# Another order of the opening among three engines, and the last expert's rows placed tile by tile at the layers' boundary and in the tail

## The chip, the cores and the metric

The kernel runs on one core of a Trainium2 chip. The time is the device time in microseconds of one execution; lower is better. In the traces PE is TensorE, DVE VectorE, ACT ScalarE, POOL GpSimd and SP the engine that issues most DMAs.

## The reference

Two layers of a decoder trunk over x (512 tokens x 1024), float32, then a final RMSNorm. Each layer is a mixer (retention and pooling branches behind one input projection) and a mixture of 16 experts, of which each token uses two; both see a normed x, scaled and shifted by rows computed from a condition c.

```python
for l in range(DEPTH):                       # DEPTH = 2
    mod = cond @ w_ada[l] + b_ada[l]
    sh1, sc1, g1, sh2, sc2, g2 = jnp.split(mod, 6, axis=-1)
    h = modulate(rmsnorm(x, norm1_g[l]), sh1, sc1)
    x = x + g1[:, None, :] * mixer(h, ...)
    h = modulate(rmsnorm(x, norm2_g[l]), sh2, sc2)
    x = x + g2[:, None, :] * moe(h, ...)     # top 2 of 16 experts, each silu(h@gate)*(h@up) @ down
return rmsnorm(x, final_g)
```

## The kernel before, in words

Tokens are four tiles of 128 rows (t = 0 to 3). Weights come as a stream of pieces of 128 x 1024 float32 (512 KB) into eight slots of `raw`. ScalarE copies a piece to `w_hi` (`hi`, L642; in experts `hi_e`, L820), VectorE subtracts it from the piece to get `w_lo` (`lo`, L989; `lo_e`, L1487), and TensorE makes each product in three passes of high and low parts (L1733 to L1735). Activations are split likewise (`unit_hi_half` L684, `unit_lo_half` L1087). `w_hi` and `w_lo` have four slots, and during the experts four more (`w_hi_more`, `w_lo_more`), which lie over `hT`. A piece of next use waits for `w_used`, the count of pieces that TensorE is done with. `LEAD` says how many pieces of an expert are converted before it begins.

Every engine has its own program in order, written by hand; what ties them together are semaphores. VectorE's `drain` waits until its own writes are in place.

Opening of layer 0: four columns of the modulation rows are products of `cond` with weights (`first_column` L2058, `first_fold` L2065) in the order 2, 0, 3, 1; the x tiles are normed in two halves of 512 columns (`first_scaled`, `first_shifted`), transposed, split (`first_hi`, `first_lo`) and multiplied with the pieces of group q (`first_product`).

Experts: each has 12 pieces, eight of gate and up (n = 0 to 7) and four of down (8 to 11), and 6 matmuls a piece. `hidden`, `hidden_transposes` and `hidT` carry the hidden rows from one to the other. `rows_out` scales an expert's output rows into `y_out` (L1510), and GpSimd stores them with an indirect DMA to `y_rows` (L2223). Of the last expert nothing is stored: its rows are added by a matmul with a 0/1-like matrix `slot_last` (transposed from `hot_last`, L1947, copied by ScalarE at L959), `last_rows_added` (L1959). What the other experts gave to each token comes back by DMA as pairs of rows (`pairs_load`, L533 to L541) once all stores have landed: `pair_early` for tiles 0 and 1, `pair_2`, `pair_3`. VectorE adds them to x (`combine`, two instructions of L1559 each); tile 2's pairs are added by TensorE (`pair_matmuls`, L1966). Then VectorE adds TensorE's sum of last rows (`last_add`, L1572) and counts `x_final`.

Boundary: x of each tile is squared and summed by ScalarE (`row_deviations`, L646, L648), normed and shifted by VectorE (`norm_tile`, L1035, L1074, L1076), transposed by TensorE (`norm_transposes`, L1818, two units of four transposes a tile), split, and multiplied with group q tile by tile (`group_tile`: 4 pieces x 2 x 3 = 24 matmuls a tile). Before, all last rows and pairs are done in one block ahead of the boundary, and the transposes of tile t + 1 stand in the middle of tile t. Tail: after layer 1 the same adds, then the final norm (`normed_output`, L1584) and the stores of `out` (L584).

## Time and profile before

| | us |
|---|---|
| median of three runs | 1492.13 (1491.58 to 1492.9) |
| the profiled execution | 1491.59 |
| its span in the trace | 1489.9 |
| PE busy | 1445.9 (97%) |
| DVE busy | 1134.2 (76%) |
| ACT busy | 773.7 (52%) |
| mean DMA rate | 253 GB/s |

The span is the time from the first to the last recorded instruction or transfer. PE's share says how much of the span TensorE had a matmul under way; what is left of it are waits. A timeline row gives start, duration, engine, line, what was written from what, how often in a row, and in square brackets the idle time before it with the instruction whose end released it.

### The profile page before, as it was taken

To read this page: it belongs to the slowest core of one execution; us is meant where nothing else is said; L and a number is where in the kernel's file an instruction comes from. 1 tells how busy PE (TensorE), PEld (TensorE's weight loads), DVE (VectorE), ACT (ScalarE), POOL (GpSimd) and SP (SyncE) were. 2 spreads that over 40 slices of the span, in tenths; PEclk is the share of its full clock that TensorE was granted. 3 is DMA by queue.
4 is the path that set the end of the run, shared out by engine and by line. 5 is a ranking of instruction groups with operands and counts; after the bars stand their busy time and mean duration, and the time that the engine had idled before them with its cause. 6 is when DMAs were issued, how large, how long until landed. Compare 5 with 4: busy or idle time off the path is not lost.

```text
span 1489.9 us, 18810 instructions
## 1 busy us (share of the span) xinstructions
PE 1445.9 (97%) x6824; PEld 1157.3 (78%) x6824; DVE 1134.2 (76%) x1531; ACT 773.7 (52%) x1102; POOL 141.6 (10%) x139
## 2 busy tenths in 40 slices
PE   6999999999999999999989999999999999999996
...
GB/s 332 296 185 200 159 220 193 147 184 161 193 210 250 386 391 387 388 389 379 313 226 197 192 141 114 194 143 89 85 171 154 295 274 394 398 387 394 380 353 190
DMA packets 107269, 377.49 MB, mean 253 GB/s; under 512 B 16505, under 2 KB 16697, under 8 KB 106404
## 3 DMA queue, kind: packets, MB, share of 16 engines
...
## 4 chain that ended last, share of the span: by engine, by line
PE 82%; DVE 12%; ACT 1%; DMA 1%; issue 1%; DVEq 1%; ACTq 0%; SPq 0%
PE ps L1733 25%; PE ps L1735 24%; PE ps L1734 24%; DVE w_lo L1487 4%; DVE w_lo_more L1487 3%; PE ps L1818 2%; PE ps L1985 1%; DMA raw<-w 1%; PE ps L1887 1%; PE ps L2032 1%; DVE xgT_lo L1476 1%; PE ps L1891 1%; DVE y_out L1510 1%; DVE w_lo L989 0%; PE ps L1959 0%
## 5 line engine op out<-in xcount | busy, mean ns | idle before, releaser
L989 DVE TENSOR_TENSOR w_lo<-raw,w_hi 128x1024 fp32r<-128x1024 f32 x134 | 163.7, 1224 | 216.6 <-ACT w_hi L642 215.2
L642 ACT ACTIVATE w_hi<-raw 128x1024 fp32r<-128x1024 f32 x134 | 141.1, 1058 | 332.8 <-PE ps L1735 332.8
L1487 DVE TENSOR_TENSOR w_lo<-raw,w_hi 128x1024 fp32r<-128x1024 f32 x192 | 229.3, 1217 | 6.1 <-ACT w_hi L820 5.0
L1733 PE MATMUL ps<-w_hi,hT_lo 128*128 128x512 f32 x512 | 206.9, 404 | 7.0 <-DVE hT_lo L1087 6.9
L820 ACT ACTIVATE w_hi<-raw 128x1024 fp32r<-128x1024 f32 x192 | 197.9, 1058 | 27.8 <-DMA raw<-w 14.8
L1487 DVE TENSOR_TENSOR w_lo_more<-raw,w_hi_more 128x1024 fp32r<-128x1024 f32 x168 | 200.5, 1216 | 2.5 <-ACT w_hi_more L820 1.6
L1735 PE MATMUL ps<-w_hi,hT_hi 128*128 128x512 f32 x512 | 201.1, 393 | 0.0
L1734 PE MATMUL ps<-w_lo,hT_hi 128*128 128x512 f32 x512 | 200.7, 392 | 0.0
L820 ACT ACTIVATE w_hi_more<-raw 128x1024 fp32r<-128x1024 f32 x168 | 172.8, 1057 | 19.2 <-DMA raw<-w 16.7
L1733 PE MATMUL ps<-hT_hi,w_lo 128*128 128x512 f32 x320 | 130.5, 408 | 0.0
L1735 PE MATMUL ps<-hT_hi,w_hi 128*128 128x512 f32 x320 | 125.0, 390 | 0.0
L1734 PE MATMUL ps<-hT_lo,w_hi 128*128 128x512 f32 x320 | 124.7, 390 | 0.0
L1733 PEld LDWEIGHTS ps<-w_hi,hT_lo 128*128 128x128 f32 x512 | 97.0, 189 | 31.7 <-DVE hT_lo L1087 9.0
L1733 PE MATMUL ps<-w_hi,xgT_lo 128*128 128x512 f32 x288 | 114.3, 397 | 3.1 <-DVE xgT_lo L1476 2.1
L1735 PEld LDWEIGHTS ps<-w_hi,hT_hi 128*128 128x128 f32 x512 | 96.8, 189 | 21.0
L1735 PE MATMUL ps<-w_hi,xgT_hi 128*128 128x512 f32 x288 | 112.4, 390 | 0.0
L1734 PE MATMUL ps<-w_lo,xgT_hi 128*128 128x512 f32 x288 | 112.3, 390 | 0.0
L1734 PEld LDWEIGHTS ps<-w_lo,hT_hi 128*128 128x128 f32 x512 | 97.0, 189 | 18.8 <-issue 0.2
L1001 DVE SCALAR_TENSOR_TENSOR ada_acc<-raw,cond,ada_acc 128x512 f32<-128x512 f32 x140 | 104.9, 749 | 6.3
L2223 POOL DMA_INDIRECT y_rows<-y_out,idx x30 | 58.0, 1932 | 436.0 <-DVE y_out L1510 418.8
L1733 PE MATMUL ps<-w_hi_more,xgT_lo 128*128 128x512 f32 x224 | 88.5, 395 | 0.0
L1735 PE MATMUL ps<-w_hi_more,xgT_hi 128*128 128x512 f32 x224 | 87.4, 390 | 0.0
...
## 6 DMA issues: line engine op xcount, KB each, us to landing
...
```

Of the source, the lines that this page charges most:

```text
L642: act.activation(w_hi[:, q % W_SLOTS], stream_piece(l, q, r), ACT.Copy).then_inc(w_hi_ready, 1)
L820: act.activation(ring_hi(r), expert_piece(e, n), ACT.Copy).then_inc(w_hi_ready, 1)
L989: v.tensor_tensor(w_lo[:, q % W_SLOTS], stream_piece(l, q, r), w_hi[:, q % W_SLOTS], ALU.subtract).then_inc(raw_used, 1)
L1001: one = v.scalar_tensor_tensor(ada_acc[:, acc], piece, c, ada_acc[:, acc], ALU.mult, ALU.add)
L1476: v.tensor_tensor(xgT_lo[:, slot, cols], ps[:, 4 + j], xgT_hi[:, slot, cols], ALU.subtract).then_inc(xgT_lo_ready, 1)
L1487: v.tensor_tensor(ring_lo(e * EXP + n), expert_piece(e, n), ring_hi(e * EXP + n), ALU.subtract).then_inc(raw_used, 1)
L1510: v.tensor_tensor(y_out[:, before % 2].rearrange("p (h n) -> p h n", h=2), ps[:, 2:4], gate_row[:].rearrange("p (h n) -> p h n", h=2), ALU ...
L1733: pe.matmul(dst, a_lo, b_hi, start=start, stop=False)
L1734: pe.matmul(dst, a_hi, b_lo, start=False, stop=False)
L1735: return pe.matmul(dst, a_hi, b_hi, start=False, stop=stop)
L1818: one = pe.transpose(bank[:, i * P:(i + 1) * P], src[:, i * P:(i + 1) * P], ident)
L2223: pool.indirect_dma_start(y_rows, bass.IndirectOffsetOnAxis(ap=idx[:, e:e + 1], axis=0), y_out[:, e % 2], None, bounds_check=2 * T - 1, oo ...
```

## The change

- Opening: ScalarE, VectorE and TensorE keep their instructions, in another order. Pieces 2 and 3 are converted earlier; column 1 is computed before product (0,2,1); the first transposes of the second half stand before product (0,3,1).
- Last expert: six instead of four of its pieces are converted during it. Its last four pieces go to ring slots 6, 7, 2, 3, so that slots 0 and 1 of `w_hi` and `w_lo` are free; in layer 0 the first two pieces of layer 1 are converted into them (`early_high`, `early_low`). `last_hot` comes earlier, the transposes of `hot_last` go into the middle of the down product, `combine` of tile 0 before `last_rows_out`.
- SP issues the first four loads of layer 1 before the pair loads; these wait for an earlier piece.
- Boundary: last rows of tiles 0 and 1 come first; pairs, the transposes of tile 0 and last rows of tile 2 next; last rows of tile 3 between the dense tiles 0 and 1. The PSUM banks of the sums change with it (`ADD_BANK`). `combine` of tiles 1 and 3 is cut into halves that stand between other steps; no `drain` and separate count follow the adds.
- Tail: the same halves of `combine`; the last tile's final norm and its store are made in two halves of 512 columns.

```diff
@@ -127,12 +127,16 @@
 RING_FROM, RING_TO = RAW_SLOTS + AHEAD, EXP * NE - W_SLOTS
-LEAD = [W_SLOTS, W_SLOTS] + [min(W_SLOTS + e - 1, 2 * W_SLOTS) for e in range(2, NE)] + [0]
+RING_END = (6, 7, 2, 3)
+LEAD = [W_SLOTS, W_SLOTS] + [min(W_SLOTS + e - 1, 2 * W_SLOTS) for e in range(2, NE - 1)] + [2 * W_SLOTS - 2, 0]
+EARLY = 2
...
-    return p % (2 * W_SLOTS) if RING_FROM <= p < RING_TO else p % W_SLOTS
+    if p >= RING_TO:
+        return RING_END[p - RING_TO]
+    return p % (2 * W_SLOTS) if p >= RING_FROM else p % W_SLOTS
...
@@ -489,8 +494,8 @@
         PAIR_DMAS = (16, 16, 16, 32)
-        ADD_BANK = (0, 4, 6, 2)
-        PAIRS_AT = 0
+        ADD_BANK = [(0, 2, 6, 6)] * (DEPTH - 1) + [(0, 2, 6, 2)]
+        PAIRS_AT = W_SLOTS
@@ -533,7 +538,7 @@
                     sp.wait_ge(row_stored[p], (l + 1) * STORED[p])
-                sp.wait_ge(w_used, w_done(l, MIX + RING_TO - W_SLOTS - 1))
+                sp.wait_ge(w_used, w_done(l, MIX + RING_TO - 7))
@@ -579,10 +584,14 @@
             pairs_load(DEPTH - 1)
-            for t in range(NT):
+            for t in range(NT - 1):
...
                 sp.dma_start(out[t * P:(t + 1) * P], x[:, t]).then_inc(out_stored, 16)
-            sp.wait_ge(out_stored, 16 * NT)
+            for half in range(2):
+                cols = slice(512 * half, 512 * half + 512)
+                sp.wait_ge(norm_done, NT + half)
+                sp.dma_start(out[(NT - 1) * P:NT * P, cols], x[:, NT - 1, cols]).then_inc(out_stored, 16)
+            sp.wait_ge(out_stored, 16 * (NT + 1))
...
@@ -640,6 +649,13 @@
                 act.activation(w_hi[:, q % W_SLOTS], stream_piece(l, q, r), ACT.Copy).then_inc(w_hi_ready, 1)
+            def early_high(l, q):
+                r = RAW_OF_W[q]
+                act.wait_ge(landed[r % RAW_SLOTS], land_value(l, r))
+                act.wait_ge(w_used, l * PROD + (q + 1) - W_SLOTS)
+                act.activation(w_hi[:, q % W_SLOTS], raw[:, r % RAW_SLOTS], ACT.Copy).then_inc(early_hi, 1)
@@ -830,14 +846,24 @@
                 if last:
+                    hi_e(next(pieces))
+                    hi_e(next(pieces))
+                    hi_e(next(pieces))
...
                     hi_e(next(pieces))
-                    hi_e(next(pieces))
                     hidT(0)
-                    hi_e(next(pieces))
+                    if l < DEPTH - 1:
+                        for q in range(EARLY):
+                            early_high(l + 1, q)
...
                     sig(1)
+                    hi_e(next(pieces))
                     hidT(1)
+                    if l < DEPTH - 1:
+                        act.drain().then_inc(w_hi_ready, EARLY)
+                    act.activation(spare[:], k("eps"), ACT.Sqrt)
+                    act.wait_ge(hot_last_turned, l + 1)
+                    act.activation(slot_last[:], ps[:, 4].rearrange("p (a b) -> p a b", a=NT), ACT.Copy).then_inc(slot_last_ready, 1)
@@ -883,33 +909,27 @@
             first_row_copy(0)
+            first_hi(0, 0)
             hi(0, 1, RAW_OF_W[1])
-            first_hi(0, 0)
...
             first_hi(0, 3)
+            hi(0, 2, RAW_OF_W[2])
             first_row_copy(3)
+            hi(0, 3, RAW_OF_W[3])
             first_row_copy(1)
-            hi(0, 2, RAW_OF_W[2])
-            first_hi(1, 0)
-            hi(0, 3, RAW_OF_W[3])
-            for t in range(1, NT):
+            for t in range(NT):
...
                 if l:
+                    for q in range(EARLY, W_SLOTS):
+                        hi(l, q, RAW_OF_W[q])
...
                         row_deviations(t)
-                        if t == 0:
-                            hi(l, 0, RAW_OF_W[0])
-                        if t == 1:
-                            hi(l, 2, RAW_OF_W[2])
-                            hi(l, 3, RAW_OF_W[3])
                         norm_hi(l, "h1", t)
-                        if t == 0:
-                            hi(l, 1, RAW_OF_W[1])
@@ -953,10 +973,8 @@
                         act.wait_ge(ov_y, b * 16 + 16)
+                        act.activation(spare[:], k("eps"), ACT.Sqrt)
                 act.nop()
-                act.activation(spare[:], k("eps"), ACT.Sqrt)
-                act.wait_ge(hot_last_turned, l + 1)
-                act.activation(slot_last[:], ps[:, 4].rearrange("p (a b) -> p a b", a=NT), ACT.Copy).then_inc(slot_last_ready, 1)
@@ -989,6 +1007,11 @@
+            def early_low(l, q):
+                v.wait_ge(early_hi, (l - 1) * EARLY + (q + 1))
+                v.tensor_tensor(w_lo[:, q % W_SLOTS], raw[:, RAW_OF_W[q] % RAW_SLOTS], w_hi[:, q % W_SLOTS], ALU.subtract)
@@ -1521,15 +1544,23 @@
                     rows_out(e - 1)
+                    lo_e(next(pieces))
+                    lo_e(next(pieces))
+                    last_hot(l)
...
                     hidT(0)
-                    lo_e(next(pieces))
+                    if l < DEPTH - 1:
+                        for q in range(EARLY):
+                            early_low(l + 1, q)
...
                     hidden(1)
+                    lo_e(next(pieces))
                     hidT(1)
-                    last_hot(l)
+                    if l < DEPTH - 1:
+                        v.drain().then_inc(raw_used, EARLY)
+                    combine(l, 0)
@@ -1559,30 +1590,25 @@
-            def combine(l, t, complete=False):
+            def combine(l, t, parts=(0, 1)):
...
                 v.wait_ge(pair_in[t], (l + 1) * PAIR_DMAS[t])
-                weighted_pair(t, w_early)
-                if complete:
-                    v.sem_inc(x_final, 1)
-            def last_add(l, t, complete=True):
+                weighted_pair(t, w_early, parts)
+            def last_add(l, t):
...
                 v.wait_ge(last_added, l * NT + (t + 1))
-                one = v.tensor_tensor(x[:, t].rearrange("p (h n) -> p h n", h=2), ps[:, ADD_BANK[t]:ADD_BANK[t] + 2],
-                                      x[:, t].rearrange("p (h n) -> p h n", h=2), ALU.add)
-                if complete:
-                    one.then_inc(x_final, 1)
-                else:
-                    v.drain()
+                v.tensor_tensor(x[:, t].rearrange("p (h n) -> p h n", h=2), ps[:, ADD_BANK[l][t]:ADD_BANK[l][t] + 2],
+                                x[:, t].rearrange("p (h n) -> p h n", h=2), ALU.add).then_inc(x_final, 1)
...
                 inverse_deviation(DEPTH * 8, t)
-                v.scalar_tensor_tensor(x[:, t], x[:, t], x_rs[:, t:t + 1], scale_row[:], ALU.mult,
-                                       ALU.mult).then_inc(norm_done, 1)
+                for cols in ([slice(0, D)] if t < NT - 1 else [slice(0, 512), slice(512, D)]):
+                    v.scalar_tensor_tensor(x[:, t, cols], x[:, t, cols], x_rs[:, t:t + 1], scale_row[:, cols], ALU.mult,
+                                           ALU.mult).then_inc(norm_done, 1)
@@ -1593,51 +1619,50 @@
                     lo(0, 0, RAW_OF_W[0])
+                    first_lo(0, 0)
                     first_shifted(0, 1)
-                    first_lo(0, 0)
...
                     first_scaled(0, 2)
+                    first_lo(0, 1)
                     first_shifted(0, 2)
-                    first_lo(0, 1)
...
                     first_part_rows(1)
+                    lo(0, 2, RAW_OF_W[2])
...
                     first_scaled(1, 0)
+                    first_shifted(1, 0)
                     first_scaled(1, 1)
-                    first_shifted(1, 0)
-                    lo(0, 2, RAW_OF_W[2])
+                    lo(0, 3, RAW_OF_W[3])
...
                     first_shifted(1, 1)
-                    lo(0, 3, RAW_OF_W[3])
                     for t in (2, 3):
+                        first_scaled(1, t)
                         first_lo(1, t - 1)
-                        first_scaled(1, t)
...
                 else:
-                    combine(l - 1, 0)
+                    combine(l - 1, 1, [0])
                     last_add(l - 1, 0)
-                    last_add(l - 1, 1, False)
+                    combine(l - 1, 1, [1])
                     norm_tile(l, 0, "h1", 0)
-                    combine(l - 1, 1, True)
-                    lo(l, 0, RAW_OF_W[0])
+                    last_add(l - 1, 1)
+                    lo(l, 2, RAW_OF_W[2])
                     norm_lo(l, "h1", 0)
-                    lo(l, 1, RAW_OF_W[1])
-                    lo(l, 2, RAW_OF_W[2])
...
                     norm_lo(l, "h1", 1)
-                    combine(l - 1, 3)
+                    combine(l - 1, 3, [0])
                     norm_tile(l, 0, "h1", 2)
+                    combine(l - 1, 3, [1])
+                    norm_lo(l, "h1", 2)
                     last_add(l - 1, 3)
-                    norm_lo(l, "h1", 2)
@@ -1711,14 +1736,15 @@
             last = DEPTH - 1
-            combine(last, 0)
+            combine(last, 1, [0])
             last_add(last, 0)
-            combine(last, 1)
+            combine(last, 1, [1])
...
             normed_output(0)
-            combine(last, 3)
+            combine(last, 3, [0])
...
             last_add(last, 2)
+            combine(last, 3, [1])
@@ -1795,7 +1821,7 @@
                 for j in range(GROUPS[g][1]):
-                    if g == 0 and t < NT - 1 and j == 2:
+                    if g == 0 and t == 1 and j == 3:
@@ -1940,30 +1966,37 @@
-            def last_rows_added(l):
+            def hot_last_turn(l):
...
                 one.then_inc(hot_last_turned, 1)
-                pe.wait_ge(slot_last_ready, l + 1)
-                pe.wait_ge(z_half, l + 1)
-                for t in range(NT):
-                    if t == 2:
-                        pe.wait_ge(pair_in[2], (l + 1) * PAIR_DMAS[2])
-                        pair_matmuls(0)
-                        pair_matmuls(1)
-                    for half in range(2):
-                        if t == 0 and half == 1:
-                            pe.wait_ge(y_copied, l * NE + (NE + 1))
-                        one = pe.matmul(ps[:, ADD_BANK[t] + half], slot_last[:, t], y_out[:, (NE - 1) % 2, 512 * half:512 * half + 512],
-                                        start=t != 2, stop=True)
-                    one.then_inc(last_added, 1)
+            def last_rows(l, t):
+                if t == 0:
+                    pe.wait_ge(slot_last_ready, l + 1)
+                    pe.wait_ge(z_half, l + 1)
+                if t == 3:
+                    pe.wait_ge(x_final, (l + 1) * NT + (3 if ADD_BANK[l][3] == ADD_BANK[l][2] else 2))
+                for half in range(2):
+                    if t == 0 and half == 1:
+                        pe.wait_ge(y_copied, l * NE + (NE + 1))
+                    one = pe.matmul(ps[:, ADD_BANK[l][t] + half], slot_last[:, t], y_out[:, (NE - 1) % 2, 512 * half:512 * half + 512],
+                                    start=t != 2, stop=True)
+                one.then_inc(last_added, 1)
+            def last_rows_pairs(l):
+                pe.wait_ge(pair_in[2], (l + 1) * PAIR_DMAS[2])
+                pair_matmuls(0)
+                pair_matmuls(1)
...
                 for half in range(2):
-                    pe.matmul(ps[:, ADD_BANK[2] + half], diag_w[:, j], pair_2[:, j, 512 * half:512 * half + 512],
+                    pe.matmul(ps[:, ADD_BANK[0][2] + half], diag_w[:, j], pair_2[:, j, 512 * half:512 * half + 512],
@@ -2019,6 +2052,8 @@
                             hidden_transposes(1)
+                            if last:
+                                hot_last_turn(l)
@@ -2086,15 +2121,15 @@
             first_transposes(0, 3)
-            first_product(0, 2, 1)
-            first_fold(3)
...
             first_column(1, [2, 3])
+            first_fold(3)
+            first_product(0, 2, 1)
+            first_fold(1)
             first_product(0, 3, 0)
-            first_fold(1)
+            first_transposes(1, 0)
             first_product(0, 3, 1)
-            first_transposes(1, 0)
@@ -2106,10 +2141,17 @@
                 if l:
+                    last_rows_pairs(l - 1)
                     norm_transposes(l, 0)
+                    last_rows(l - 1, 2)
...
                         group_tile(l, 0, t)
+                        if t == 0:
+                            norm_transposes(l, 1)
+                            last_rows(l - 1, 3)
+                        if t == 2:
+                            norm_transposes(l, 3)
@@ -2153,6 +2195,7 @@
                     pe.wait_ge(y_copied, l * NE + (NE + 1))
+                    pe.wait_ge(slot_last_ready, l + 1)
@@ -2184,7 +2227,12 @@
                 pe.nop()
-                last_rows_added(l)
+                last_rows(l, 0)
+                last_rows(l, 1)
+                if l == DEPTH - 1:
+                    last_rows_pairs(l)
+                    last_rows(l, 2)
+                    last_rows(l, 3)
```

## Rows read from the trace of the kernel before

**Rows 1.** The page: busy time of TensorE; the chain that ended last, by engine.
```profile
PE 1445.9 (97%) x6824; PEld 1157.3 (78%) x6824; DVE 1134.2 (76%) x1531; ACT 773.7 (52%) x1102; POOL 141.6 (10%) x139
...
PE 82%; DVE 12%; ACT 1%; DMA 1%; issue 1%; DVEq 1%; ACTq 0%; SPq 0%
```
**Rows 2.** Waits of TensorE over the whole span: total us, times, longest.
```profile
PE ps L1733 <- DVE hT_lo L1087: 6.9, 3, 2.5
...
PE ps L1818 <- DVE h_nat L1076: 3.9, 1, 3.9
PE ps L2032 <- DVE hid L1493: 3.0, 9, 0.7
...
PE ps L1733 <- DVE hidT_lo L1499: 0.9, 3, 0.3
```
**Rows 3.** Timeline of TensorE in the opening: start, duration, operation, idle before.
```profile
25.00 0.50 PE L1733 MATMUL ps<-w_hi,hT_lo 128*128 128x512 f32 x1 [2.19 <-DVE hT_lo L1087]
...
47.96 0.50 PE L1733 MATMUL ps<-w_hi,hT_lo 128*128 128x512 f32 x1 [2.45 <-DVE hT_lo L1087]
```
**Rows 4.** Timelines of ScalarE and of SP's DMA issues in the opening.
```profile
22.68 1.05 ACT L642 ACTIVATE w_hi<-first_w 128x1024 fp32r<-128x1024 f32 x1
...
44.50 0.60 ACT L870 ACTIVATE shift_row<-ps 128x512 f32<-128x512 f32 x1 [4.48 <-DVE h_nat L1059]
45.00 1.05 ACT L642 ACTIVATE w_hi<-raw 128x1024 fp32r<-128x1024 f32 x1
...
35.15 7.01 SPq L522 DMA_DIRECT2D raw<-w  x6
```
**Rows 5.** Timeline of TensorE at the boundary between the layers.
```profile
744.03 3.70 PE L1959 MATMUL ps<-y_out,slot_last 128*128 128x512 f32 x8 [0.69 <-ACT slot_last L959]
...
757.71 0.50 PE L1733 MATMUL ps<-w_hi,hT_lo 128*128 128x512 f32 x1 [2.24 <-DVE hT_lo L1087]
...
764.63 1.97 PE L1818 MATMUL ps<-const,h_nat 128*128 128x128 f32 x8 [3.88 <-DVE h_nat L1076]
...
781.09 0.48 PE L1733 MATMUL ps<-w_hi,hT_lo 128*128 128x512 f32 x1
...
789.12 0.39 PE L1735 MATMUL ps<-w_hi,hT_hi 128*128 128x512 f32 x1
```
**Rows 6.** Busy time by stretch; then granted clock, DMA share and GB/s.
```profile
764.00:768.00 4.00, 3.37 (x12) 3.08 (x13) 3.14 (x5) 1.96 (x3) 0.00 (x0) 0.50 0.40 152
768.00:772.00 4.00, 4.00 (x14) 3.11 (x14) 3.35 (x4) 0.56 (x3) 0.00 (x0) 0.72 0.01 2
```
**Rows 7.** VectorE: timeline at the boundary, then groups with mean ns of one.
```profile
744.15 2.64 DVE L1559 SCALAR_TENSOR_TENSOR x<-pair_early,w_early,x 128x1024 f32<-128x1024 f32 x2
...
751.34 1.23 DVE L1076 TENSOR_TENSOR h_nat<-h_nat,shift_row 128x1024 f32<-128x1024 f32 x1
...
L1572 DVE TENSOR_TENSOR x<-ps,x 128x1024 f32<-128x1024 f32 x8 | 9.6, 1219 | 0.2
...
L1487 DVE TENSOR_TENSOR w_lo<-raw,w_hi 128x1024 fp32r<-128x1024 f32 x192 | 229.3, 1217 | 6.1 <-ACT w_hi L820 5.0
```
**Rows 8.** Pair loads of layer 0 with their landing; GpSimd's timeline of row stores.
```profile
L538 SPq DMA_DIRECT2D pair_early<-y_rows x2: 381/426/471, 733.3 to 733.7; - x2
...
DMA to landing us min/median/max: 4.7/5.8/6.9
...
714.42 2.66 POOL L2223 DMA_INDIRECT y_rows<-y_out,idx  x1 [15.04 <-DVE y_out L1510]
729.86 0.96 POOL L2223 DMA_INDIRECT y_rows<-y_out,idx  x1 [12.78 <-DVE y_out L1510]
```
**Rows 9.** Timeline of VectorE in the tail.
```profile
1467.78 2.65 DVE L1559 SCALAR_TENSOR_TENSOR x<-pair_early,w_early,x 128x1024 f32<-128x1024 f32 x2
...
1483.86 0.16 DVE L1035 RECIPROCAL x_rs<-x_std 128x1 f32<-128x1 f32 x1 [0.45 <-ACT x_std L648]
...
1485.53 1.28 DVE L1584 SCALAR_TENSOR_TENSOR x<-x,x_rs,scale_row 128x1024 f32<-128x1024 f32 x1
```

5 lines of the change are left out of this document (3 added, 2 removed).

## The prediction

> **What bounds the kernel now.** I read the page first: TensorE is busy for 97% of the span and carries 82% of the chain that ended last, VectorE 12% [rows 1]. So TensorE's work sets the time, except where it waits and where it has finished. The change adds and removes no matmul, so all it can move is idle time of TensorE, half-clock time of TensorE, and the piece of VectorE's work behind the last matmul. The list of TensorE's waits [rows 2] shows what there is: 6.9 us for `hT_lo` and 3.9 us for `h_nat`, both of the opening and of the boundary between the layers, and small ones of the last expert (`hid`, `hidT_lo`). The timelines then place them. Times below are positions in the profiled execution.
>
> **Opening.** Two waits stand before first uses of `hT_lo`: 2.19 us until 25.00 and 2.45 us until 47.96 [rows 3].
> - The first. ScalarE converts piece 1 (22.68, 1.05 us) before it copies the first transposed unit; VectorE likewise makes `h_nat` of tile 1 before its own half of that unit [rows 4]. The edit turns both around. The transposes end near 22.8, ScalarE's copy of 0.6 us then ends near 23.55, VectorE's subtract of 0.7 near 24.25, and the first product starts at 24.3: 0.7 us gained. Piece 1 is then converted by 24.55 and its low part by 26.0; it is needed after two transposes and six matmuls, near 26.4. Nothing is late.
> - The second. ScalarE copies the shift row at 44.50, then piece 2 at 45.00 [rows 4], then the transposed unit; VectorE repeats that order with 1.22 us for the low part. In the new kernel pieces 2 and 3 are converted while ScalarE waits for column 3 and column 1 anyway (it is idle 4.5 us before 44.50), and TensorE runs column 1 before product (0,2,1) and puts product (0,3,1) behind the transposes. I lay the new order out from 36.2: column 1 (1.9 us) to 38.0, fold 3 to 38.9, product (0,2,1) to 40.3, fold 1 to 41.2, product (0,3,0) to 42.6, transposes to 43.0, product (0,3,1) to 44.35. VectorE is ready with the unit's low half at 44.8, so the next product starts at 44.85 against 47.96: 3.1 us in all, the first 0.7 among them. The weak point is piece 2: SP issues its load when column 3's third piece is used, 34.4 in the new order (35.15 before [rows 4]). It needs to land by 38; behind it in ScalarE's queue stands the copy of the scale row, and behind that the whole second half. Bounds for this part: 0.7 (the load is late) to 3.8 (VectorE never late). I take 3.1.
>
> **Last expert, both layers.** Two of expert 14's conversions move behind `rows_out`, so expert 14's rows are scaled 2.3 us earlier (two of 1.217 [rows 7]). `hidT_lo` no longer stands behind two conversions: its three waits add up to 0.9 us [rows 2], of which 0.5 in the tail, and there the wait for `hid` (0.26 of the 3.0) goes too. The four transposes of `hot_last` (0.6 us) move between the matmuls of the down product; they are issued in either case, but now `slot_last` is copied long before it is needed. In layer 0 the two early conversions cost VectorE 2 x 1.217 in the same place, so `hidden(1)` ends at 738.4 as now and the down product at 742.8 as now: nothing gained, nothing lost. In the tail they are absent, and the down product ends 0.85 us earlier.
>
> **Boundary.** Now: the last rows and pairs are three blocks like the one at 744.03, 3.4 us each, up to 754.4; then transposes, 2.24 us wait, half of a dense tile, 3.88 us wait for the next `h_nat`, and then matmuls at half clock: the granted clock is 0.50 in 764 to 768 and 0.72 in 768 to 772 [rows 5, 6]. The group ends at 789.3. A matmul costs (789.12 - 781.09) / 35 = 0.229 us at full clock, a tile of 24 costs 5.5.
> The new order, from the down product's end at 742.8. VectorE: combine of tile 0 (two of 1.32 us [rows 7]) lies before `last_rows_out`, in a place where it now waits for TensorE's last product; `last_rows_out` ends at 744.15 as now; then half of combine 1 to 745.4, last add 0 (1.219 less overlap, 1.15) to 746.65, ScalarE's deviation 1.6 us beside the other half of combine 1, norm of tile 0 to 751.2 (now 752.57 [rows 7]), last add 1 to 752.3, low part of piece 2 to 753.45, `norm_lo` to 754.7. TensorE: last rows 0 and 1 from 743.7 (0.3 earlier, it waits for the first half of `y_out` only) to 747.15, pairs to 750.6, 0.7 idle, transposes 0 to 752.2, last rows 2 to 753.9, 0.85 idle, dense tile 0 from 754.75 to 760.2 (now from 757.71). Transposes 1 need the norm of tile 1, ready 758.7: no wait. Last rows 3 (1.7 us) need last add 2, done 759.8: no wait, and they cover `norm_lo` of tile 1. Tile 1 runs 762.9 to 769.25 with transposes 2 in it, 0.4 idle, tile 2 to 775.1, transposes 3, then 1.75 idle, since nothing is left to cover the copy and subtract of tile 3, and tile 3 to 783.3. Against 789.3 this is 6.0 us. It is made of 3.88 us wait, some 2.7 us of half clock (nine matmuls and eight transposes at twice their time), 1.0 us at the first tile's wait and 0.3 at its start, less 2.1 new idle time. Behind the boundary TensorE works without waits, so the gain stays. Bounds: 3.0 (the half clock comes back, a link of VectorE's chain is late) to 7.
>
> **What the moved loads do.** In layer 0 SP now issues four weight loads before the pair loads, behind which the row store of expert 14 has to find its way. Pair tile 0 takes 4.7 us to land from an issue at 733.3 [rows 8]; the combine before `last_rows_out` wants it at 740.0. The row store is issued 2.3 us earlier, but VectorE goes on at once with conversions of two SBUF inputs: the same store takes 2.66 us at 714.42, where VectorE is busy, and 0.96 at 729.86, where it idles [rows 8]. With 2.66 and one more us for the loads in front, the pairs are issued at 733.8 and tile 0 lands at 738.5: 1.5 us in hand. The Trainium skill ("SBUF — State Buffer", Who interferes with whom) says that GpSimd and VectorE take turns at a shared port pair, the second blocked in full; the trace agrees as far as these two rows go. By the 0.96 alone the landing would be at 736.8; the sum is the same by either.
>
> **Tail.** VectorE's chain runs from 1467.78 to 1486.81 [rows 9]. Removed: combine of tile 0, 2.65 us, which moves ahead of `last_rows_out`. Added: three tenths, as last add 0 now waits for its matmuls. Earlier start: 0.85. Interleaving the halves of combine 1 and 3 hides ScalarE's deviations; the 0.45 us wait for `x_std` [rows 9] shrinks to 0.1. The last normalisation in two halves costs 0.2 more on VectorE. Sum: 2.65 + 0.85 + 0.35 = 3.85 with the two small costs cancelled by waits inside the chain. The final store is 256 KB instead of 512: from VectorE's end to the span's end it is 1489.9 - 1486.8 = 3.1 us now, and I take 0.3 off. Tail: 4.2, bounds 2.5 to 5.5.
>
> **Sum.** 3.1 + 6.0 + 4.2 = 13.3 us. The profiled execution took 1491.59 us (span 1489.9); the median shown is 1492.13, 0.54 above. Predicted: 1492.1 - 13.3 = 1478.8.
>
> **Rivals.**
> 1. *The half clock comes back at the boundary.* TensorE has 0.7 and 0.85 us idle around transposes and last rows, then 1.75 before tile 3. Now it goes 2.24 us idle without a drop and drops after 3.88 more [rows 5, 6]; that speaks against it. Price: 0.2 us on each of some ten to twenty matmuls, 2 to 4 us: 1480.8 to 1482.8. Chance 10%. The Trainium skill ("TensorE: Matmul & The Clock Gate", Part 1) says that the array runs at 1.2 GHz until activity releases 2.4 GHz and falls back when idle.
> 2. *The pair loads are late in layer 0.* If the row store lands as late as under a full queue, pair tile 0 lands near 743 and VectorE, which works in order, is 3 us late with `last_rows_out`; TensorE idles as long and may lose the clock too. 1481.8 to 1484. Chance 15%.
> 3. *The opening gains only its first step*, because the load of piece 2 holds up the scale row: 1481.2. Chance 12%.
> 4. *Slower.* The same queue as in 2, with pair tile 0 so late that `last_rows_out` waits out the whole gain. It decides from a landing at about 751.5 on: 11.5 us behind the need plus 2 of half clock is 13.3. The landings seen reach 6.9 us for these tiles [rows 8], so a landing 18 us after its issue would be new. 1494 or more. Chance 4%.
> 5. *The change does not do what it says*: VectorE's sum over the boundary and tail is the same work and only waits change places, some 4 us stay: 1488. Speaks against it: 2.65 us really leave the stretch behind the last matmul in each layer. Chance 6%; half of it within 0.2%.
>
> Forecast itself 53%. Its range is 1476.5 to 1481; with rivals 1 to 3 it reaches to 1485. I give 1476 to 1485. A measurement tells about 0.2% (3 us) from no change. Chances: faster 0.93, same 0.03, slower 0.04.
>
> **What would show it.** In the profile after: the first L1733 matmul at 24.3 and the second half's first at about 44.9; no wait on `h_nat` over 1 us at the boundary, granted clock 1.00 from 764 on, and the q group ended near 780 on its own clock (783.3 less the opening's 3.1); a wait of 1.5 to 2 us before the last tile's products; VectorE busy with `x<-pair_early` before the last `y_out` in both layers; VectorE's last instruction some 16 us after the last `y_out` instead of 19.0. Wrong if a load (`pair_early`, or `raw` in the opening) is named as releaser of VectorE or ScalarE, or if the waits of layer 1 grow by what the boundary gave.

## The result, and the profile after

| | before | after |
|---|---|---|
| median, beside each other on one chip | 1492.52 us (4 runs) | 1479.07 us (1478.23 to 1479.38, 4 runs) |
| ratio, 95% interval | | 0.9908 (0.9891 to 0.9925) |
| the profiled execution, span | 1491.59, 1489.9 | 1479.38, 1477.8 |

Predicted were 1478.8 us. The profiled executions differ by 12.2 us, the medians by 13.4. TensorE's busy time falls by 3.5 us with the same 6824 matmuls (more of them ran at half clock before). The profile's page of after answers to [rows 1]:

```profile
PE 1442.4 (98%) x6824; PEld 1155.0 (78%) x6824; DVE 1133.3 (77%) x1532; ACT 773.2 (52%) x1102; POOL 143.4 (10%) x139
```

Waits of TensorE in after, against [rows 2] (L1759 is L1733 of before, L1844 is L1818, L2067 is L2032):

```profile
PE ps L1759 <- DVE hT_lo L1110: 4.1, 5, 1.6
PE ps L2067 <- DVE hid L1516: 3.3, 8, 0.8
...
PE ps L1986 <- DVE y_out L1541: 1.7, 2, 0.9
...
PE ps L1917 <- ACT state L713: 1.2, 1, 1.2
...
PE ps L1844 <- DVE h_nat L1099: 0.6, 1, 0.6
```

The 3.9 us for `h_nat` became 0.6, and 2.8 of the 6.9 for `hT_lo` went. New are small waits for `y_out`. One for `state` in layer 0's retention grew from 0.5 to 1.2 us, though the change touches nothing there; it comes back below.

Opening, TensorE of after, against [rows 3]:

```profile
23.70 0.50 PE L1759 MATMUL ps<-w_hi,hT_lo 128*128 128x512 f32 x1 [1.41 <-DVE hT_lo L1110]
...
44.49 0.50 PE L1759 MATMUL ps<-w_hi,hT_lo 128*128 128x512 f32 x1 [0.27 <-DVE hT_lo L1110]
```

and ScalarE of after, with piece 2 (38.13) and the scale row, against [rows 4]:

```profile
38.13 1.06 ACT L651 ACTIVATE w_hi<-raw 128x1024 fp32r<-128x1024 f32 x1 [1.65 <-DMA raw<-w]
39.10 0.58 ACT L896 ACTIVATE scale_row<-ps 128x512 f32<-128x512 f32 x1
```

ScalarE waited for the load of piece 2 until 38.1, the very time at which the layout wanted it. The copy of the scale row stands directly behind, 0.3 us later than column 3's sum would have allowed; the shift row was copied at 41.97.

Boundary, TensorE of after, against [rows 5]; the windows below against [rows 6]:

```profile
741.15 3.67 PE L1986 MATMUL ps<-y_out,slot_last 128*128 128x512 f32 x8 [0.87 <-DVE y_out L1541]
...
748.90 1.09 PE L1844 MATMUL ps<-const,h_nat 128*128 128x128 f32 x8 [0.64 <-DVE h_nat L1099]
...
752.36 0.50 PE L1759 MATMUL ps<-w_hi,hT_lo 128*128 128x512 f32 x1 [0.65 <-DVE hT_lo L1110]
...
767.42 0.51 PE L1759 MATMUL ps<-w_hi,hT_lo 128*128 128x512 f32 x1 [0.18 <-DVE hT_lo L1110]
...
775.69 0.50 PE L1759 MATMUL ps<-w_hi,hT_lo 128*128 128x512 f32 x1 [1.57 <-DVE hT_lo L1110]
...
781.04 0.39 PE L1761 MATMUL ps<-w_hi,hT_hi 128*128 128x512 f32 x1
```

```profile
764.00:768.00 4.00, 3.82 (x22) 2.81 (x21) 3.82 (x5) 1.08 (x2) 0.00 (x0) 1.00 0.00 0
768.00:772.00 4.00, 4.00 (x19) 3.34 (x18) 2.20 (x4) 1.45 (x3) 1.71 (x3) 1.00 0.48 197
```

The waits stand where the layout put them, 0.64, 0.65, 0.18 and 1.57 us where 0.7, 0.85, 0.4 and 1.75 were forecast, and the clock stays at 1.00 (1.00 is full clock, 0.50 half). The group ends at 781.04 instead of 789.12.

Row stores and pair loads of after, against [rows 8], and VectorE with `combine` ahead of the last `y_out`, against [rows 7]:

```profile
725.11 1.19 POOL L2271 DMA_INDIRECT y_rows<-y_out,idx  x1 [10.51 <-DVE y_out L1533]
```

```profile
731.64 0.90 SPq L543 DMA_DIRECT2D pair_early<-y_rows  x2
```

```profile
737.27 2.66 DVE L1590 SCALAR_TENSOR_TENSOR x<-pair_early,w_early,x 128x1024 f32<-128x1024 f32 x2
740.32 1.29 DVE L1541 TENSOR_TENSOR y_out<-ps,gate_row 128x512 f32<-128x512 f32 x2 [0.39 <-PE ps L1761]
```

Tail, VectorE of after, against [rows 9]:

```profile
1454.20 2.64 DVE L1590 SCALAR_TENSOR_TENSOR x<-pair_early,w_early,x 128x1024 f32<-128x1024 f32 x2
1457.48 1.29 DVE L1541 TENSOR_TENSOR y_out<-ps,gate_row 128x512 f32<-128x512 f32 x2 [0.63 <-PE ps L1761]
...
1473.68 1.42 DVE L1610 SCALAR_TENSOR_TENSOR x<-x,x_rs,scale_row 128x512 f32<-128x512 f32 x2
```

From the end of `y_out` (1458.77) to VectorE's last it is 16.3 us; before it was 1486.81 - 1467.86 = 18.95.

### The profile page after: what moved, and what is told of

Same layout as the page of the kernel before. It is cut to its first block, busy times and chain, and to the rows that moved or that the text cites. A ratio compares the mean times of both kernels' runs of the same rounds, so it can differ in the third digit from the quotient of the medians.

```text
span 1477.8 us, 18814 instructions
## 1 busy us (share of the span) xinstructions
PE 1442.4 (98%) x6824; PEld 1155.0 (78%) x6824; DVE 1133.3 (77%) x1532; ACT 773.2 (52%) x1102; POOL 143.4 (10%) x139
## 4 chain that ended last, share of the span: by engine, by line
PE 83%; DVE 11%; DMA 2%; ACT 1%; issue 1%; DVEq 1%; ACTq 0%; SPq 0%
PE ps L1759 25%; PE ps L1761 24%; PE ps L1760 24%; DVE w_lo L1510 3%; DVE w_lo_more L1510 3%; DMA raw<-w 2%; PE ps L1844 2%; PE ps L2018 1%; PE ps L1913 1%; PE ps L2067 1%; PE ps L1917 1%; DVE xgT_lo L1499 1%; DVE y_out L1533 1%; DVE w_lo L1007 1%; PE ps L1948 0%
## 5 line engine op out<-in xcount | busy, mean ns | idle before, releaser
L1007 DVE TENSOR_TENSOR w_lo<-raw,w_hi 128x1024 fp32r<-128x1024 f32 x132 | 161.3, 1224 | 213.9 <-ACT w_hi L651 212.6
L651 ACT ACTIVATE w_hi<-raw 128x1024 fp32r<-128x1024 f32 x132 | 139.1, 1058 | 334.2 <-PE ps L1761 332.5
L1510 DVE TENSOR_TENSOR w_lo<-raw,w_hi 128x1024 fp32r<-128x1024 f32 x188 | 224.2, 1216 | 3.9 <-ACT w_hi L836 3.0
L1759 PE MATMUL ps<-w_hi,hT_lo 128*128 128x512 f32 x512 | 206.6, 404 | 4.1 <-DVE hT_lo L1110 4.1
L1510 DVE TENSOR_TENSOR w_lo_more<-raw,w_hi_more 128x1024 fp32r<-128x1024 f32 x172 | 205.2, 1216 | 2.4 <-ACT w_hi_more L836 1.3
L836 ACT ACTIVATE w_hi<-raw 128x1024 fp32r<-128x1024 f32 x188 | 193.5, 1058 | 24.5 <-DMA raw<-w 15.1
L836 ACT ACTIVATE w_hi_more<-raw 128x1024 fp32r<-128x1024 f32 x172 | 177.0, 1057 | 25.2 <-DMA raw<-w 15.7
L1759 PE MATMUL ps<-hT_hi,w_lo 128*128 128x512 f32 x320 | 130.5, 408 | 0.0
L1759 PEld LDWEIGHTS ps<-w_hi,hT_lo 128*128 128x128 f32 x512 | 96.4, 188 | 30.3 <-DVE hT_lo L1110 8.3
L1759 PE MATMUL ps<-w_hi,xgT_lo 128*128 128x512 f32 x288 | 114.3, 397 | 3.2 <-DVE xgT_lo L1499 2.1
L1759 PE MATMUL ps<-w_hi_more,xgT_lo 128*128 128x512 f32 x224 | 88.5, 395 | 0.0
## 6 DMA issues: line engine op xcount, KB each, us to landing
x_state<-x POOLq DMA_DIRECT2D x2, 2048.0 KB, 10.1
y_rows<-x_in ACTq DMA_DIRECT2D x4, 1024.0 KB, 12.5
```

What stands on the lines that cost most here:

```text
L651: act.activation(w_hi[:, q % W_SLOTS], stream_piece(l, q, r), ACT.Copy).then_inc(w_hi_ready, 1)
L836: act.activation(ring_hi(r), expert_piece(e, n), ACT.Copy).then_inc(w_hi_ready, 1)
L1007: v.tensor_tensor(w_lo[:, q % W_SLOTS], stream_piece(l, q, r), w_hi[:, q % W_SLOTS], ALU.subtract).then_inc(raw_used, 1)
L1510: v.tensor_tensor(ring_lo(e * EXP + n), expert_piece(e, n), ring_hi(e * EXP + n), ALU.subtract).then_inc(raw_used, 1)
L1759: pe.matmul(dst, a_lo, b_hi, start=start, stop=False)
```

## Experiments

Each ratio below is to before on the same chip. The times of before for the three groups of runs are 1491.77 (first four kernels below), 1492.04 (`e_comb_late`, `e_comb_first`, `e_t1_mid`, `e_pairs_first`) and 1492.55 (the rest). Positions of the opening vary between executions with the first loads, so I count them from the first transposes.

**The opening alone, and all but the opening.** `e_open` is before with the three engines' new order of the opening (the hunks of `first_...`, `hi(0, ...)` and `lo(0, ...)` in the diff of the change), `e_noopen` is after with the old one; no other line differs. `e_swap` is before with the two swaps ahead of the first product only:

```diff
+            first_hi(0, 0)
             hi(0, 1, RAW_OF_W[1])
-            first_hi(0, 0)
...
+                    first_lo(0, 0)
                     first_shifted(0, 1)
-                    first_lo(0, 0)
```

> The kernel before with the new opening alone (boundary, last expert and tail as before). Theory: 0.7 us at the first product and 3.1 us at the second half's first product (from 47.96 to near 44.9), of which the retention stage takes back about 0.75, as in the profile of the changed kernel (its wait for ScalarE's state grew from 0.47 to 1.23 us): 1490.1. Rival 1, the retention stage takes nothing back in this kernel: 1489.4. Rival 2, part of the shift in the changed kernel's profile (0.5 us, already there at 17.9) is variation of the loads and not of the order: then the VectorE reciprocal of tile 1 stands at 18.4 here again and not at 17.9.

> The changed kernel with the opening of before. If the parts add up, it is slower than the changed kernel by what the opening gives, 2.4 to 3.1 us: 1481.5 to 1482.2, and boundary and tail keep their 5.4 and 4.0 us. The retention stage's wait for the state is back at 0.5 us if the new opening made it grow, and stays at 1.2 if it varies by itself. Rival: opening and boundary gains overlap (something in between is bound by the loads), then it is less than 1 us slower than the changed kernel: 1479.5 to 1480.

> The kernel before with one edit: ScalarE copies the first transposed unit before it converts piece 1, VectorE makes the unit's low half before the shift of tile 1. Theory: the first dense product starts 0.7 us earlier (24.3 against 25.0) and the second half's first product too (47.3). Rival: what follows waits for piece 1 (then the second product's group starts at 27.5 as before and nothing is left): look at the wait before it.

Measured: `e_open` 1488.32 (0.9974, 0.9964 to 0.9984), 3.5 us less than before and better than both times expected. `e_noopen` 1481.63 (0.9932, 0.9919 to 0.9946), 10.1 less than before. `e_swap`, one run, 1490.19; single runs of before lie between 1490.27 and 1494.11, so this time alone says little. The timelines of TensorE, first of `e_open`, then of `e_noopen`:

```profile
21.70 0.66 PE L1817 MATMUL ps<-const,h_nat 128*128 128x128 f32 x4 [0.78 <-DVE h_nat L1058]
23.77 0.50 PE L1732 MATMUL ps<-w_hi,hT_lo 128*128 128x512 f32 x1 [1.41 <-DVE hT_lo L1086]
...
43.14 0.50 PE L1732 MATMUL ps<-w_hi,hT_lo 128*128 128x512 f32 x1
```

```profile
22.09 0.65 PE L1845 MATMUL ps<-const,h_nat 128*128 128x128 f32 x4 [0.78 <-DVE h_nat L1083]
24.94 0.50 PE L1760 MATMUL ps<-w_hi,hT_lo 128*128 128x512 f32 x1 [2.19 <-DVE hT_lo L1111]
...
46.60 0.50 PE L1760 MATMUL ps<-w_hi,hT_lo 128*128 128x512 f32 x1 [2.45 <-DVE hT_lo L1111]
```

From the transposes to the second half it is 43.14 - 21.70 = 21.44 us in the new order and 46.60 - 22.09 = 24.51 in the old: 3.1, of which 2.85 - 2.07 = 0.8 before the first product. The medians of the opening and of the rest add up: 3.5 and 10.1 make 13.6. In `e_swap` the 0.8 is there at the first product too, but TensorE then waits 0.50 us for the next `hT_lo`, and at the second half (45.90 - 21.65 = 24.25) 0.3 is left: the first step alone gives little.

The 3.1 is not the whole of it. Behind the 2.45 us wait of the old order the clock can fall, as in `e_noopen`:

```profile
48.00:52.00 4.00, 4.00 (x16) 3.19 (x15) 1.81 (x4) 0.60 (x1) 0.00 (x0) 0.65 0.99 417
```

Up to the last transposes of the opening `e_noopen` takes 56.41 - 22.09 = 34.3 us and `e_open` 51.64 - 21.70 = 29.9, a difference of 4.4. Before and after, which both had half clock near 24 to 28 instead, differ by 34.3 - 31.4 = 2.9 at that place. The 3.5 of the medians lies between these two.

**Is the half clock at the boundary a cost of its own?** `e_fill` gives TensorE useless matmuls in the gap before the transposes of tile 1; their output is overwritten later, all of the reference's work is done.

```diff
                     if g == 0 and t < NT - 1 and j == 2:
+                        if t == 0:
+                            for _ in range(19):
+                                pe.matmul(ps[:, 1], ones_r[:], ones_r[:].unsqueeze(1).broadcast_to([P, 4, P]), start=True, stop=True)
                         norm_transposes(l, t + 1)
```

> The kernel before, with 19 matmuls of no use into a free bank put before the transposes of tile 1 at the boundary, where TensorE waits 3.88 us for h_nat. They lengthen nothing that is needed as long as they end before h_nat is ready. Theory: the stall costs more than its length, because the granted clock is 0.50 for 4 us behind it; with the fillers it stays at 1.00 and the eight transposes and nine to ten matmuls after it take half: 2.0 to 2.7 us less, 1489.8 to 1490.5. Rival: VectorE's chain sets the end of this stretch, so a faster TensorE only waits more at the next tile: 1492.0 to 1492.5.

Measured: 1493.16, 1.4 us slower than before (1.0013, 1.0004 to 1.0022). TensorE of `e_fill`, its fillers and transposes:

```profile
760.75 4.48 PE L1801 MATMUL ps<-ones_r 128*128 128x512 f32 x19
765.07 1.04 PE L1821 MATMUL ps<-const,h_nat 128*128 128x128 f32 x8
...
773.56 1.09 PE L1821 MATMUL ps<-const,h_nat 128*128 128x128 f32 x8 [2.00 <-DVE h_nat L1076]
...
781.57 1.04 PE L1821 MATMUL ps<-const,h_nat 128*128 128x128 f32 x8
```

and its windows:

```profile
764.00:768.00 4.00, 4.00 (x24) 3.39 (x23) 3.56 (x5) 2.22 (x5) 0.00 (x0) 1.00 0.37 133
...
772.00:776.00 4.00, 2.44 (x12) 2.15 (x13) 3.68 (x5) 1.75 (x3) 0.78 (x2) 0.83 0.00 0
776.00:780.00 4.00, 4.00 (x15) 3.15 (x14) 2.85 (x4) 0.67 (x3) 0.93 (x2) 0.75 0.96 393
```

In before, the last two of these groups of transposes, and VectorE's `h_nat` of tile 2:

```profile
773.89 1.10 PE L1818 MATMUL ps<-const,h_nat 128*128 128x128 f32 x8
...
780.30 1.03 PE L1818 MATMUL ps<-const,h_nat 128*128 128x128 f32 x8
```

```profile
772.61 1.23 DVE L1076 TENSOR_TENSOR h_nat<-h_nat,shift_row 128x1024 f32<-128x1024 f32 x1
```

With the fillers the clock is 1.00 from 764 to 768 and the eight transposes take half as long, yet the next ones can't start before VectorE has `h_nat` of tile 2, in before at 772.61 + 1.23 = 773.84. Nearly all that TensorE saved comes back as 2.00 us of waiting. Behind that wait the clock falls, and tile 3's transposes follow 8.0 us later instead of 6.4; this second fall is what makes the run slower.

VectorE's chain does hold a small part of the half clock. It can split tile 1 only once the transposes are done and ScalarE has copied them; first before, then `e_fill`:

```profile
766.41 0.69 DVE L1087 TENSOR_TENSOR hT_lo<-ps,hT_hi 128x512 fp32r<-128x512 f32 x1 [0.70 <-ACT hT_hi L684]
```

```profile
766.34 1.29 DVE L1087 TENSOR_TENSOR hT_lo<-ps,hT_hi 128x512 fp32r<-128x512 f32 x2 [0.44 <-ACT hT_hi L684]
```

Counted from the last rows, tile 2's transposes start after 773.89 - 744.03 = 29.86 us in before and 773.56 - 744.22 = 29.34 in `e_fill`: 0.5 us earlier, although the fillers let tile 1's transposes begin 0.25 late. `e_swap` shows the rest without any fillers. There the eight transposes ran at half clock too, but the clock was back after three matmuls instead of nine; TensorE finished 1.3 us sooner and waited:

```profile
772.71 1.10 PE L1818 MATMUL ps<-const,h_nat 128*128 128x128 f32 x8 [1.34 <-DVE h_nat L1076]
```

From the last rows that is 772.71 - 742.84 = 29.87, as in before. So of the 2.7 us of half clock in before some 0.5 to 0.8, that of the transposes, was a cost, and that of the matmuls was none.

**What is the moved `combine` worth?** `e_comb_late` is after with it put back; `e_comb_first` is before with it moved alone.

```diff
-                    combine(l, 0)
                     last_rows_out()
+                    combine(l, 0)
```

```diff
                     last_hot(l)
+                    combine(l, 0)
                     last_rows_out()
...
-                    combine(l - 1, 0)
                     last_add(l - 1, 0)
...
-            combine(last, 0)
             last_add(last, 0)
```

> The changed kernel, but VectorE combines tile 0 behind last_rows_out again, in both layers. Theory (VectorE's chain sets the end at the boundary and in the tail): last add 0 stands 2.3 us later at both places (combine 2.65 and the half of combine 1, less the 0.35 that it waited for its matmuls), the first dense tile starts 2.3 us later, and all of it reaches the end: 4.6 us more than the changed kernel's 1479.1, 1483.7. Rival (TensorE's order sets the end, the chain has slack): under 1 us more, 1479 to 1480.

> The kernel before with that one move: VectorE combines tile 0 ahead of last_rows_out. It stands behind last_hot here, so last_rows_out starts 0.9 us late (about 743.8 for 742.9); 2.65 - 0.9 = 1.75 us are left at each of two places. If VectorE's chain sets the end in both: 3.5 us less than the kernel before on the same chip (1491.8), 1488.3. If at the boundary only TensorE's stall and its half clock count and they fall as they like: 1.75 from the tail alone, 1490.0.

Measured: `e_comb_late` 1484.85 (0.9953, 0.994 to 0.9967), some 6 us above after. `e_comb_first` 1493.25 (1.0006, 0.9997 to 1.0015): no gain. TensorE of `e_comb_late`:

```profile
741.43 3.67 PE L1986 MATMUL ps<-y_out,slot_last 128*128 128x512 f32 x8 [0.88 <-DVE y_out L1541]
...
752.20 1.16 PE L1844 MATMUL ps<-const,h_nat 128*128 128x128 f32 x8 [3.66 <-DVE h_nat L1099]
...
779.73 0.50 PE L1759 MATMUL ps<-w_hi,hT_lo 128*128 128x512 f32 x1 [1.57 <-DVE hT_lo L1110]
```

and VectorE of `e_comb_first`:

```profile
741.38 2.65 DVE L1560 SCALAR_TENSOR_TENSOR x<-pair_early,w_early,x 128x1024 f32<-128x1024 f32 x2
744.17 1.29 DVE L1518 TENSOR_TENSOR y_out<-ps,gate_row 128x512 f32<-128x512 f32 x2
747.01 1.23 DVE L1573 TENSOR_TENSOR x<-ps,x 128x1024 f32<-128x1024 f32 x1 [1.54 <-PE ps L1958]
```

Put back, it delays the transposes of tile 0 by 3.0 us (a wait of 3.66 instead of 0.64) and with them the last tile: from the last rows it starts 38.3 us later, in after 34.5. That is 3.8 in this boundary: 2.65 for the instructions, 0.4 more up to the transposes, and 0.7 behind them, where the granted clock is 0.64 from 752 to 756. From the start of `y_out` to the span's end it is 23.2 us against 20.3: 2.9 in the tail. Moved alone, it gains nothing: `y_out` starts at 744.17 instead of 742.94, 1.0 us late once the 0.27 is taken off by which this execution came to the down product later, and the first `last_add` waits 1.54 for matmuls that used to run beside the `combine`: 2.5 of the 2.65 us are gone. The change puts two things around the move that meet just these two losses: `last_hot` and `slot_last` early, so that `combine` ends before the down product, and half of `combine` 1 as cover for the last rows' matmuls. That is read from the traces; no run has the one without the other. Of the 10.1 us outside the opening some 6 hang on this place of `combine`; the other 4 (the order of the last rows on TensorE, the halves of the other `combine`s, no `drain` behind the adds) were not taken apart further.

**Three more placements.** `e_t1_mid` is after with the transposes of tile 1 in the middle of tile 0, as before; `e_pairs_first` is after with the pair loads ahead of layer 1's weights in SP's queue; `e_noearly` is after without the early conversions, all four pieces being converted at the boundary.

```diff
+                    if g == 0 and t == 0 and j == 2:
+                        norm_transposes(l, 1)
...
                         if t == 0:
-                            norm_transposes(l, 1)
                             last_rows(l - 1, 3)
```

```diff
-        PAIRS_AT = W_SLOTS
+        PAIRS_AT = 0
```

```diff
...
-                    if l < DEPTH - 1:
-                        for q in range(EARLY):
-                            early_low(l + 1, q)
...
-                    lo(l, 2, RAW_OF_W[2])
+                    lo(l, 0, RAW_OF_W[0])
                     norm_lo(l, "h1", 0)
+                    lo(l, 1, RAW_OF_W[1])
+                    lo(l, 2, RAW_OF_W[2])
                     lo(l, 3, RAW_OF_W[3])
```

> The changed kernel with the transposes of tile 1 back in the middle of dense tile 0 (last rows of tile 3 stay behind tile 0). In the changed kernel TensorE reaches that place at 755.1 and h_nat of tile 1 is ready at 756.1: a new wait of 1.0 us. Theory A (TensorE's order is what gives): the wait goes through to the end, 1480.1. Theory B (VectorE's chain sets the end, as the run with fillers showed for the kernel before): norm_lo of tile 1 is done earlier and the chain behind it is not later, the 1.57 us idle ahead of the last tile takes the wait up, 1479.1, and that idle is near 0.6 us.

> The changed kernel with the pair loads ahead of layer 1's first four loads again. The early conversion of piece 0 stands in ScalarE's queue in the middle of the last expert and now waits for a load that is issued behind 4 MB of pairs, near 734 and landing near 746; hi(190), silu and the hidden rows stand behind it. Theory: ScalarE waits some 13 us for raw, TensorE as long for hid, and its clock drops: 12 to 16 us slower than the changed kernel, 1491 to 1495. Rival: the row store, no longer behind four loads, lands 2.5 us earlier and so do the pairs and the load: 9 to 11 us.

> The changed kernel without early conversions: pieces 0 and 1 of layer 1 are converted at the boundary, the loads stay ahead of the pairs. VectorE saves 2.4 us in the last expert of layer 0, so hidden(1) no longer waits and the down product ends 0.5 to 0.9 us earlier; at the boundary the low parts of pieces 0 to 3 take 2.4 us more of VectorE's chain between last add 1 and the norm of tile 1. If VectorE's chain sets the end: 1.5 to 2 us slower than the changed kernel, 1480.6 to 1481.1. If TensorE's order does: 0.5 to 0.9 faster, 1478.3.

Measured: `e_t1_mid` 1478.38 (0.9906, 0.989 to 0.9921), `e_pairs_first` 1491.96 in one run, `e_noearly` 1478.9 (0.9912, 0.9899 to 0.9926). TensorE of the three, in this order:

```profile
740.00 3.67 PE L1988 MATMUL ps<-y_out,slot_last 128*128 128x512 f32 x8 [0.88 <-DVE y_out L1541]
...
755.08 1.09 PE L1846 MATMUL ps<-const,h_nat 128*128 128x128 f32 x8 [0.85 <-DVE h_nat L1099]
...
775.50 0.50 PE L1759 MATMUL ps<-w_hi,hT_lo 128*128 128x512 f32 x1 [1.57 <-DVE hT_lo L1110]
```

```profile
746.30 0.69 PE L2067 MATMUL ps<-const,hid 128*128 128x128 f32 x2 [12.50 <-DVE hid L1516]
```

```profile
737.73 3.67 PE L1978 MATMUL ps<-y_out,slot_last 128*128 128x512 f32 x8 [1.36 <-DVE y_out L1536]
...
773.21 0.50 PE L1751 MATMUL ps<-w_hi,hT_lo 128*128 128x512 f32 x1 [1.57 <-DVE hT_lo L1105]
```

From last rows to the last tile it is 34.5 us in after, 35.5 in `e_t1_mid` and in `e_noearly`. So each placement costs 1.0 in its boundary. For `e_t1_mid` the profiled executions differ by 0.9 (1479.3 against 1478.36 of `e_after_again`), the medians by 0.1; whether the 1.0 reaches the total stays open.

`e_noearly` has most of its 1.0 back ahead of the boundary. Beside `e_after_again` its last row store is 2.0 us earlier (722.03 against 724.05), which no early conversion explains: its opening had no half clock, and some waits for `hid` were shorter. Without VectorE's two conversions the down product then ends 2.8 earlier, another 0.8. But the last rows start only 2.4 earlier (737.73 against 740.09), because VectorE's `combine` waits for the pairs and `y_out` is late. So the early conversions cost 0.8 us in the last expert and give 1.0 at the boundary, and the medians, 1478.9 against 1478.31, don't tell the two kernels apart.

The late load is not a matter of this variant alone. `e_whole_store`, which is the changed kernel up to the tail, shows it too; first `e_noearly`, then `e_whole_store`:

```profile
734.09 2.66 DVE L1580 SCALAR_TENSOR_TENSOR x<-pair_early,w_early,x 128x1024 f32<-128x1024 f32 x2 [0.86 <-DMA pair_early<-y_rows]
```

```profile
735.63 2.66 DVE L1586 SCALAR_TENSOR_TENSOR x<-pair_early,w_early,x 128x1024 f32<-128x1024 f32 x2 [0.64 <-DMA pair_early<-y_rows]
```

In `e_whole_store` TensorE's wait for `y_out` is 1.13 us by it, instead of 0.88.

`e_pairs_first` shows what the new order of SP's queue is for. The early conversions stand in ScalarE's and VectorE's order between the last expert's steps; if their loads wait behind the pairs, and these behind the row store, everything stands still for 12.5 us. The pair loads themselves go 2.67 us after the store's end there (724.89 to 727.56), and 5.3 in after.

**Store, fills, and after again.** `e_whole_store` keeps the last tile's norm and store in one piece:

```diff
...
-                for cols in ([slice(0, D)] if t < NT - 1 else [slice(0, 512), slice(512, D)]):
+                for cols in [slice(0, D)]:
```

`e_fills_spread` issues ScalarE's four DMAs that fill `y_rows` one by one behind the projections `g0`, `g1`, `ap0` and `R0`, where ScalarE waits anyway, instead of all in the retention:

```diff
-                    if l == 0:
-                        for t in range(NT):
-                            act.dma_start(y_tiles[t], x_in[:, t * D:(t + 1) * D].unsqueeze(1).broadcast_to([P, 2, D])).then_inc(y_filled, 16)
...
+                if l == 0 and name in ("g0", "g1", "ap0", "R0"):
+                    t = ("g0", "g1", "ap0", "R0").index(name)
+                    act.dma_start(y_tiles[t], x_in[:, t * D:(t + 1) * D].unsqueeze(1).broadcast_to([P, 2, D])).then_inc(y_filled, 16)
```

> The changed kernel with the last tile's final norm and store in one piece. Theory: from VectorE's end to the end of the span 3.1 us again instead of 2.7, and VectorE's last instruction ends 0.15 us earlier: 0.25 us slower, 1479.3. Rival: two stores cost their own fixed time and the whole one is as fast: 1479.0. The difference is below what the times can tell; the two positions in the profile decide.

> The changed kernel with the four fills of y_rows, which ScalarE issues in a row ahead of the retention of layer 0 (4.62 us in the changed kernel, 3.86 before), issued one at a time behind groups g0, g1, ap0 and R0. Theory: TensorE's wait for the first state (1.23 us in the changed kernel's profile, 0.47 before) goes, nothing else moves: 1478.0 to 1478.6. Rival: an issue costs ScalarE 0.6 to 1 us wherever it stands and holds up a gate or a conversion there: same or slower, 1479 to 1480.

> The changed kernel itself, beside the three on the same chip: 1479.1. Its profile also tells what varies by itself: the half-clock stretch of the opening near 24 to 28, the wait for the first state (0.5 to 1.2), and the position of the first transposes (21.6 to 22.6).

Measured, side by side: after again 1478.31 (1478.21 to 1478.69; 0.9907), `e_whole_store` 1478.26 (1477.27 to 1479.29; 0.9906), `e_fills_spread` 1477.58 (1476.49 to 1478.26; 0.9901, 0.9886 to 0.9916). From the start of `y_out` to the span's end the profiles have 20.24 us in two pieces (1456.46 to 1476.7) and 20.56 in one (1456.14 to 1476.7): the split store is worth 0.3, too little for the medians. The four fills take 4.62 us of ScalarE's queue in the profile of after and 3.86 in that of before, and TensorE waits 1.2 and 0.5 us for `state` behind them. In the profiles of after again and of `e_whole_store` it doesn't wait at all; there they take 2.68 and 2.88. So this wait comes and goes between executions. In the one profile of `e_fills_spread` it is absent, as the spreading would have it, but that one profile can't tell this from chance; the 0.7 us in the medians is no more than the runs spread. `e_fills_spread` is the quickest of all, by a margin that these runs don't secure.

## Why the prediction was right

**Opening: 3.1 forecast, 3.1 shown.** The first product is 0.8 earlier (0.7 forecast), the second half 3.1, by `e_open` against `e_noopen`; after against before gives 25.81 - 22.86 = 2.95. Product one of the second half started at 44.49, forecast 44.85; half a microsecond of this is earlier loads. The weak point named, the load of piece 2, was as tight as computed (38.13 against "by 38"). The prediction's own sign of being wrong, a load named as releaser of ScalarE, stands in that row (1.65 us, `raw<-w`). It cost little: the scale row was copied 0.3 us late and TensorE waited 0.27 at 44.49. In `e_t1_mid`, whose opening is the same and ran at full clock, the load released ScalarE 0.8 too late for the scale row, TensorE waited 0.52, and the second half started 22.10 us after the first transposes instead of 21.44. Rival 3, only the first step gained, is refuted by both runs. By the medians the opening alone is worth 3.5. The 0.4 above the forecast fits the half clock behind the old order's second wait (`e_noopen`), for which the forecast had no term.

**Last expert.** The down product of layer 0 neither gains nor loses: TensorE came to it 2.7 us earlier than before, by the opening less the retention, and the last `y_out` starts 2.6 earlier (742.94 against 740.32). In `e_noearly` it ends 0.8 earlier, near the 0.85 that the prediction had for the tail, where there are no early conversions.

**Boundary: 6.0 forecast, 5.4 shown** (789.12 - 781.04 = 8.08, less 2.7 with which TensorE came in). The layout of the new order was right to 0.3 us at each wait. The sum as I explained it (its terms make 5.8) was not: 3.88 wait plus 2.7 half clock is no pair of independent gains. Of the 2.7, `e_fill` and `e_swap` show 0.5 to 0.8 as a cost. What the boundary of before lasts is VectorE's chain up to `h_nat` of tile 2 at 773.84, and the gain is what leaves that chain or gets covered in it: the `combine` (`e_comb_late`: 3.8), the two early conversions and the place of tile 1's transposes (1.0 each), and waits for deviations. These were each taken out of the changed kernel alone and need not add up to 5.4. The layout was safe from this error because it followed VectorE, step by step, and did not use the list of gains; the forecast rests on the layout, so the number is no luck, but the reason given beside it was wrong. Of the 0.6 that are missing, 0.2 is the end of the group in before (789.12, where the sum had 789.3); the rest, on the clock of before, is tile 0 at 752.36 + 2.7 = 755.06 instead of 754.75 and the end at 783.74 instead of 783.3. VectorE's 0.35 us wait for the first last rows stood in no term of the layout.

**Loads in layer 0.** Two terms were mis-sized and cancelled: the row store took 1.19 us on GpSimd, not 2.66, though VectorE was busy all the while (`w_lo` from 724.26 to 726.61); and its landing, seen as SP's next issue, came 5.3 us after its end instead of 2.5 + 1. The pairs were issued at 731.64 on a clock that was 2.7 early, where 733.8 was forecast on the clock of before: 734.3 on that clock, half a microsecond late, with 0.9 us in hand of the 1.5. That the two errors nearly cancel is luck. Rival 2 did not come true in after, but its start is seen in the same code: in `e_whole_store` the landing took 6.8 us, the pairs were 0.64 us late and `y_out` 0.25; in `e_noearly`, where VectorE is ready earlier, they were 0.86 late. This too is a sign that the prediction had named, a load as releaser of VectorE; the margin of 1.5 us was in truth between 0.9 and nothing. The store before that one, under `w_lo` conversions of VectorE too, took 2.67:

```profile
711.94 2.67 POOL L2271 DMA_INDIRECT y_rows<-y_out,idx  x1 [15.06 <-DVE y_out L1533]
```

The Trainium skill ("SBUF — State Buffer", Who interferes with whom) says that a VectorE instruction with two SBUF inputs contends with a GpSimd instruction that reads SBUF. The 2.67 here fits that, the 1.19 of 725.11, under the same kind of conversions, does not, so these rows leave the length of such an issue unexplained. What hangs on it is 1.5 us of landing.

**Tail: 4.2 forecast, 4.0 shown.** At expert 15's first hidden transposes TensorE is 1456.15 - 1448.02 = 8.1 us ahead of before, at the span's end 12.1. VectorE's stretch behind `y_out` is 2.6 shorter (3.0 forecast), the store 0.4 (0.3 forecast), and the expert itself gave 1.0 (0.85), as `y_out` starts 9.1 earlier.

**The sum.** In the profiled executions the opening gave 2.95 and earlier loads 0.5, and the retention took 0.75 back (the wait for `state` 1.23 against 0.47): 2.7. With 5.4 and 4.0 this is the 12.1 by which the spans differ. Without the wait for `state`, as in after again, the times differ by 1491.59 - 1478.36 = 13.2. Rival 1 (half clock back) is refuted by the windows (1.00 all through the boundary in after and in every variant but `e_comb_late` that keeps its order), rival 5 by `e_open` and `e_comb_late`, rival 4 by the landing. How easily all of the gain can go is seen in `e_pairs_first`, though by late weight loads and not by late pairs: the same parts with one constant of before give 1491.96 in its one run, no gain at all.
